# Scoring the first query tile against its own 128 keys, and adding a head's squares on VectorE before the ones-product

## The reference, cut to what matters

```
h = rmsnorm(x) * (1 + sc1) + sh1                 # sc1, sh1, ... = silu(c) @ w_ada + b_ada
proj = h @ w_in                                  # GLA q, k, v, gate; MoBA q, k, v; two branch gates
o_gla  = rmsnorm(gla(q, k, v, log_a)) * silu(gr) # 4 heads, dv = 256
o_moba = softmax(mask(q @ k.T * 128**-0.5)) @ v  # 8 heads x 128; 256 tokens are one block: plain causal
y = (sigmoid(gate_a) * (o_gla @ w_gla_out) + sigmoid(gate_b) * (o_moba @ w_moba_out)) @ w_o
x = x + gt1 * rmsnorm(y)
x = x + gt2 * rmsnorm(conv_ffn(rmsnorm(x) * (1 + sc2) + sh2))
```

## Time and profile before

| | |
|---|---|
| runs | 1500.78, 1501.9, 1497.0 us; median 1500.78 us |
| profiled execution | 1505.08 us, its span 1503.2 us |
| PE busy | 1442.4 us, 96% of the span |
| DVE busy | 1108.0 us, 74% |
| ACT busy | 756.1 us, 50% |
| POOL busy | 84.4 us, 6% |
| memory | 367 MB moved, mean 244 GB/s |

### The profile page before, as it was taken

How to read it: one execution, slowest core, us unless ns; L and a number is a source line. 1 busy time by engine, 2 the same in 40 slices (tenths; PEclk the granted TensorE clock), 3 DMA queues, 4 the chain that set the end, 5 groups by cost and what they waited for, 6 DMA issues and landing times.

```text
span 1503.2 us, 19959 instructions
## 1 busy us (share of the span) xinstructions
PE 1442.4 (96%) x7386; PEld 1231.6 (82%) x7386; DVE 1108.0 (74%) x1119; ACT 756.1 (50%) x743; POOL 84.4 (6%) x176
## 2 busy tenths in 40 slices
PE   2989999999999999999789999999999999999997
PEld 2777888888888888868678888888888888888886
DVE  5989978889898988855577778778777666545554
ACT  4443443353545365424566665665665665444443
POOL 3000001110101100000000000000000000000000
PEclk9999999999999999999989999999999999999999
DMA  9999979797989877866547677577765555555553
GB/s 361 387 329 354 313 230 327 243 308 260 304 265 299 266 253 254 305 227 235 168 168 237 225 237 236 194 240 236 236 237 184 191 180 193 192 195 195 195 195 112
DMA packets 235526, 367.03 MB, mean 244 GB/s; under 512 B 11455, under 2 KB 161473, under 8 KB 234706
## 3 DMA queue, kind: packets, MB, share of 16 engines
q1 hardware_dynamic: 215536, 294.69, 58.9%
q0 software_dynamic: 18848, 69.23, 12.8%
q10 hardware_dynamic: 1090, 2.40, 0.4%
HBM read 364.18 MB, written 2.10 MB: 244 GB/s over the span
## 4 chain that ended last, share of the span: by engine, by line
PE 82%; DVE 7%; DMA 7%; issue 2%; ACT 2%; SPq 0%; DVEq 0%
PE ps L1154 82%; DMA ada<-in_w_ada 3%; DVE lo L697 2%; DMA raw<-in_w_in 1%; DVE acc L707 1%; DVE acc_a L726 1%; ACT hi L426 1%; DMA adar<-in_w_ada 1%; DMA raw<-in_w_moba_out 1%; DVE acc_b L726 0%; DMA raw<-in_w_up 0%; DVE GA L817 0%; PE ps L1361 0%; DVE yo L1026 0%; DVE yt L1026 0%
## 5 line engine op out<-in xcount | busy, mean ns | idle before, releaser
L1154 PE MATMUL ps<-hT,hi 128*128 128x512 f32 x1936 | 469.0, 395 | 2.0 <-DVE hT L1066 2.0
L1154 PEld LDWEIGHTS ps<-hT,hi 128*128 128x128 f32 x1936 | 358.4, 189 | 74.1 <-issue 3.2
L426 ACT ACTIVATE hi<-raw 128x2048 fp32r<-128x2048 f32 x117 | 224.1, 1915 | 290.9 <-DMA raw<-in_w_in 192.9
L697 DVE TENSOR_TENSOR lo<-raw,hi 128x2048 fp32r<-128x2048 f32 x117 | 267.2, 2285 | 74.3 <-ACT hi L426 74.3
L1154 PEld LDWEIGHTS ps<-hT,lo 128*128 128x128 f32 x1936 | 248.2, 191 | 9.4
L1154 PE MATMUL ps<-hT,lo 128*128 128x256 f32 x1936 | 251.1, 283 | 0.0
L1115 DVE TENSOR_TENSOR lo<-raw,hi 128x2048 fp32r<-128x2048 f32 x88 | 200.1, 2291 | 50.1 <-ACT hi L658 50.0
L1154 PE MATMUL ps<-hi,hT 128*128 128x512 f32 x768 | 187.4, 397 | 8.2 <-DVE hT L751 5.7
L1154 PEld LDWEIGHTS ps<-hi,hT 128*128 128x128 f32 x768 | 144.5, 191 | 39.1 <-issue 9.0
L1154 PE MATMUL ps<-hi,asp 128*128 128x512 f32 x704 | 173.9, 389 | 0.0
L658 ACT ACTIVATE hi<-raw 128x2048 fp32r<-128x2048 f32 x88 | 166.2, 1906 | 4.4 <-DMA raw<-in_w_up 3.2
(11 more groups left out here) (199 smaller groups left out, 1334.9 us busy)
## 6 DMA issues: line engine op xcount, KB each, us to landing
raw<-in_w_up SPq DMA_DIRECT2D x176, 512.0 KB, 4.4
raw<-in_w_in SPq DMA_DIRECT2D x162, 512.0 KB, 5.6
ada<-in_w_ada POOLq DMA_DIRECT2D x128, 512.0 KB, 4.9
raw<-in_w_down SPq DMA_DIRECT2D x88, 512.0 KB, 4.1
adar<-in_w_ada SPq DMA_DIRECT2D x64, 512.0 KB, 9.7
raw<-in_w_o SPq DMA_DIRECT2D x32, 512.0 KB, 4.8
raw<-in_w_gla_out SPq DMA_DIRECT2D x16, 512.0 KB, 4.9
raw<-in_w_moba_out SPq DMA_DIRECT2D x16, 512.0 KB, 5.2
```

What stands on the lines that cost most here:

```text
L426: act.activation(hi[:, w % 4, :], raw[:, w % 4, :], ACT.Copy).then_inc(hi_done, 1)
L697: dve.tensor_tensor(lo[:, w % 4, :], raw[:, w % 4, :], hi[:, w % 4, :].bitcast(F32), ALU.subtract).then_inc(lo_done, 1)
L1154: return pe.matmul(out_, lhsT, rhs, start=start, stop=stop)
```

## The change

The scores of query tile 0 are computed against keys 0 to 127 alone. In `ssb` and in the bank a head now has 384 columns in place of 512: columns 0 to 127 for query tile 0, 128 to 383 for query tile 1 (`score_cols`). The mask is laid out anew, the row maximum is two instructions per `hd`, and the exponential, the scaling and the transposes follow the new columns. Apart from that, DVE adds the second half of the squares to the first in its tail at n = 0, and PE multiplies ones with that sum once. PE waits there for the new semaphore `sq_sum`, which DVE counts up, where it waited for ACT's `sq_done`.

```diff
+        def score_cols(qt):
+            return slice(0, P) if qt == 0 else slice(P, 3 * P)
...
             made(pool.memset(causal[:, :], 0.0))
-            cv4 = causal[:, :].rearrange("p (t k) -> p t k", t=TT)
-            made(pool.affine_select(out=cv4, in_=cv4, compare_op=ALU.is_ge, fill=-1e30, base=0,
-                                    pattern=[[P, TT], [-1, TOK]], channel_multiplier=1))
+            diagonal = causal[:, :].rearrange("p (t k) -> p t k", t=TT)[:, :, 0:P]
+            made(pool.affine_select(out=diagonal, in_=diagonal, compare_op=ALU.is_ge, fill=-1e30, base=0,
+                                    pattern=[[0, TT], [-1, P]], channel_multiplier=1))
...
                             for qt in range(TT):
-                                v = ssb[:, hd, TOK * qt:TOK * (qt + 1)]
+                                v = ssb[:, hd, score_cols(qt)]
                                 j = 2 * hd + qt
                                 act.activation(v, v, ACT.Exp, scale=SCALE, bias=stat[:, 20 + j:21 + j],
...
             def tail(prev, n):
+                if n == 0:
+                    dve.wait_ge(sq_done, prev + 1)
+                    dve.tensor_tensor(sq[:, 0, :], sq[:, 0, :], sq[:, 1, :], ALU.add).then_inc(sq_sum, 1)
                 if n == 1:
...
-                            link(dve.tensor_tensor(ssb[:, hd, :], ps[:, 6 + hd, :], causal[:, :], ALU.add))
-                            link(dve.reduce_max(stat[:, 16 + 2 * hd:18 + 2 * hd],
-                                                ssb[:, hd, :].rearrange("p (t k) -> p t k", t=TT), AX.X), wait=hd == 1)
+                            link(dve.tensor_tensor(ssb[:, hd, 0:3 * P], ps[:, 6 + hd, 0:3 * P], causal[:, 0:3 * P], ALU.add))
+                            for qt in range(TT):
+                                link(dve.reduce_max(stat[:, 16 + 2 * hd + qt:17 + 2 * hd + qt], ssb[:, hd, score_cols(qt)], AX.X),
+                                     wait=hd == 1 and qt == 1)
...
-                                v = ssb[:, hd, TOK * qt:TOK * (qt + 1)]
+                                v = ssb[:, hd, score_cols(qt)]
                                 j = 28 + 2 * hd + qt
                                 ins = dve.tensor_scalar(v, v, stat[:, j:j + 1], None, ALU.mult)
...
-                        for j, (qt, k) in enumerate(((0, 0), (1, 0), (1, 1))):
-                            ins = pe.transpose(ps[:, 6 + hd, P * j:P * (j + 1)],
-                                               ssb[:, hd, TOK * qt + P * k:TOK * qt + P * (k + 1)], ident[:, :])
+                        for j in range(3):
+                            ins = pe.transpose(ps[:, 6 + hd, P * j:P * (j + 1)], ssb[:, hd, P * j:P * (j + 1)], ident[:, :])
                         ins.then_inc(pt_done, 1)
-                    pe.wait_ge(sq_done, prev + 1)
-                    mm(ps[:, 5, 0:TOK], ones[:, :], sq[:, 0, :], True, False)
-                    mm(ps[:, 5, 0:TOK], ones[:, :], sq[:, 1, :], False, True).then_inc(ss_done, 1)
+                    pe.wait_ge(sq_sum, prev + 1)
+                    mm(ps[:, 5, 0:TOK], ones[:, :], sq[:, 0, :]).then_inc(ss_done, 1)
...
-                                ins = mm(ps[:, 6 + hd, TOK * qt:TOK * (qt + 1)], mqk[:, 0, hd, P * qt:P * (qt + 1)], mqk[:, 1, hd, :])
+                                ins = mm(ps[:, 6 + hd, score_cols(qt)], mqk[:, 0, hd, P * qt:P * (qt + 1)], mqk[:, 1, hd, 0:P * (qt + 1)])
```

More of the change, by code:

```diff
@@ L214, in layer_kernel @@
         cross, evac, vm_evac = sems("cross evac vm_evac")
-        e_ready, exp_done, level_ready, gram_done, select_done, a01_done = sems(
-            "e_ready exp_done level_ready gram_done select_done a01_done")
+        sq_sum, e_ready, exp_done, level_ready, gram_done, select_done, a01_done = sems(
+            "sq_sum e_ready exp_done level_ready gram_done select_done a01_done")
         av_done, ot_done, sq_done, ss_done, rs_done, tanh_done, og_f = sems(
```

## The result

The changed kernel takes 1521.52 us (median of 5 runs, 1519.97 to 1522.22) against 1500.78 us before (5 runs, 1497.0 to 1506.31): 20.7 us more, ratio 1.0112, 95% interval 1.0086 to 1.0139. The forecast was 1519.3 us. That the kernel is slower is clear of noise; by how much is known to a few us.

What follows compares the result with a forecast made beforehand. PE was taken to bound the kernel, DVE close behind. 16.5 us of waiting plus 4.5 of low clock less 2.5 of PE's work gave 18.5 us more: 1519.3 us median, 8 in 10 within 1509 to 1525 us.

Steps and rivals of the forecast that it cites:

- The wait: At each of the first three borders PE waits 5.5 us for DVE's sum of squares, 16.5 us in all.
- DVE's lateness: At the first three borders DVE reaches the add's place 5.34 us after PE wants the sum.
- DVE's shorter score work: Mask adds, row maxima and scalings on DVE before the border take 0.55 us less per head.
- No wait at the merge: At the border to the merge DVE's add is done about 1.8 us before PE wants it.
- The clock: PE's clock falls to half level at each of three border waits, costing 1.5 us each, 4.5 us in all.
- PE's saving: Shorter score products (0.24 us) and one ones-product fewer (0.38 us) save PE 0.62 us a head, 2.5 us in all.
- The rule that I had set aside: PE's score products: matmul distance proportional to columns alone would save 0.40 us a head, 3.1 us in the sum.
- The clock holds: Rival, chance 0.10: border stalls come without the 4.5 us of low clock; 14.0 us more, 1514.8 us.
- DVE keeps its lead: Rival, chance 0.07: only the first border stalls; 4.5 us more, 1505.3 us.
- PE is held there anyway: Rival, 0.06 with "The add comes in time": another wait already holds PE at the border product, only the difference costs.
- The add comes in time: Rival, 0.06 with "PE is held there anyway": border lateness falls under about 0.6 us, PE's saving remains, 1498.3 us.

Runs made afterwards that it cites:

- the repeat: The changed kernel itself, unaltered, timed again beside a kernel with 40 filling matmuls: 1522.4 us (6 runs), ratio 1.0123.
- the squares alone: Kernel before with only the edit to the sum: DVE adds the halves at n = 0, PE waits for it; 1522.8 us, ratio 1.0129.
- the scores alone: Changed kernel with the sum put back to two ones-products behind ACT's squares, shorter scores kept: 1501.16 us, ratio 0.9988.
- one border: Changed kernel with the sum on DVE at the first border only, two products at the others: 1508.21 us, ratio 1.0028.
- moved units: Changed kernel with three ada units per head (heads 0 to 2) moved from before the border to behind n = 3, 4, 5: 1500.59 us, ratio 0.999.
- the filled waits: Changed kernel with unused matmuls before PE's wait at three borders: 34 gave 1518.35 us, ratio 1.0097; 40 gave 1521.68 us, ratio 1.01.

## Why the prediction was right, and what was mis-sized

The mechanism came as forecast: three waits of nearly equal length, none at the merge, DVE's lead gone in each head. The number is within its range partly because the errors of the terms cancel: 0.6 us too much for the waits, 2.2 too little for the clock, 0.7 too little for the saving. With the measured terms the sum is 15.9 + 6.7 - 3.2 = 19.4 us, against 20.7 between the medians.

**The wait.** Forecast 3 x 5.5 = 16.5 us, measured 15.9 in the first profile, 15.3 in the repeat and 16.5 with the squares alone. The add takes 0.42 us as worked out from its neighbours, DVE's shorter score work gives 0.47 us a head (mask adds and maxima to the next instruction 2.35 us in place of 2.76, scalings to the split 0.98 in place of 1.04) where I had 0.55, and PE arrives 0.41 us earlier in place of 0.24. These would make 5.75 us a border; the mean is 5.3, so the term that was too large is the 5.34 of DVE's lateness. It isn't a constant: with the scores alone DVE starts the split of n = 0 at 4.6, 5.5 and 4.6 us behind PE's last transpose, where the kernel before has 5.3 each time. That the earlier trace rows agreed to 0.02 us was luck. The wait came three times, since DVE meets ACT's copy and PE again in each head; that the lateness comes from the units in front of the border, and that one border alone costs a third, the runs with moved units and with one border show. No wait at the merge: the add is done at 574.5, PE comes at 576.43.

**The clock.** This term was too small: 4.5 us forecast, 6.7 measured, 6.5 and 8.1 in the profiles of the repeated run and of the squares alone. The clock was low for about 3.4 us in the earlier trace rows, from 650.7 us on, all of it behind the wait. Here it was low from 327.2 to 334.1, from 412.6 to 416.0 and from 494.5 to 501.3 us: twice as long at two of the three borders (at two in the repeat, at all three with the squares alone). It did begin before the restart, by 0.3 to 2.2 us, as I had reckoned, but lasted 6.2, 3.1 and 4.6 us beyond it. Why some stretches are twice as long, the runs don't show. The page of the Trainium skill "TensorE: Matmul & The Clock Gate", section "HAM oscillation — how this bites in real kernels", has waits between bursts put each next burst at half rate; at all nine borders of the three profiles the trace agrees. As a part of the run time it is read from profiles; the filled waits confirm that it is there, and not its size.

**PE's saving.** Mis-sized too, by little. The eight loads of `mqk` now take 1.21 us to the next group, 0.15 each where I expected 0.17:

```profile
301.73 1.18 PEld L1161 LDWEIGHTS ps<-mqk 128*128 128x128 f32 x8
302.94 3.17 PEld L1161 LDWEIGHTS ps<-hT,hi 128*128 128x128 f32 x14
```

Against the 1.62 us of the earlier trace rows that is 0.41 us a head, the upper bound, since the products of `Mb` in the earlier trace rows were no price for these. With 0.41 for the scores and 0.38 for the product the saving is 3.2 us in place of 2.5. The rule that I had set aside, distance in proportion to the columns (the Trainium skill, page "TensorE: Matmul & The Clock Gate", section "Back-to-back issue gap"), gives 0.40; the trace has 0.41.

**The sum.** From the scores alone to the changed kernel the merge begins 21.8 us later (548.50 and 570.32): 15.9 of waiting + 6.7 of clock - 3 x 0.38 for the products = 21.5. From the kernel before it is only 18.3 us, because its profiled execution had a fall of the clock in the first head that the changed one hadn't, for 1.7 us, and because the kernel before lacks the 1.6 us that the scores save:

```profile
264.00:266.00 2.00, 2.00 (x9) 1.54 (x9) 2.00 (x3) 1.61 (x3) 0.00 (x0) 0.75 1.02 308
266.00:268.00 2.00, 2.00 (x6) 1.63 (x5) 2.00 (x4) 1.25 (x2) 0.00 (x0) 0.50 0.82 286
268.00:270.00 2.00, 2.00 (x12) 1.74 (x12) 2.00 (x6) 1.01 (x2) 0.53 (x1) 0.90 0.36 99
```

The rest of the way takes 951.2 us before and 949.3 after; nothing of size is given back there.

**The rivals.** "The clock holds" is wrong in every profile of the changed kernel. "DVE keeps its lead" and "PE is held there anyway" are wrong. "The add comes in time" is wrong here, and true with three units moved, where the waits are 0.5 us a border on average, under the 0.6 us of its condition.

## What to carry to other kernels

An engine can be late by most of a tile at no cost until another one asks it for something there. Before a small piece of work is moved from the bounding engine to one with idle time, look up in the timeline when the new engine reaches the very place in its queue and when the result is wanted; if it is late, move the piece ahead of the long work, which here made the same instructions 20 us cheaper. Saving 1.5 us of products is not worth a wait on an engine that itself waits for transfers.

## What the hardware showed beyond that

Waits of equal length end with and without a fall of the clock. In the first head the kernel before waits for `Mb` for 2.0 us and the clock falls at 265.0 us, 1.4 us after the restart; the changed kernel waits for 2.2 us at the same place and it holds. The wait of 2.97 us of the earlier trace rows had no fall; the same wait in the changed kernel, 2.92 us up to 761.3 us, has one that begins at 760.7. With the 2.83 us of the earlier trace rows, which had a fall, no length between 2 and 3 us tells the outcome. The nine waits at the borders, 4.4 to 5.7 us in the profiles of the changed kernel, its repeat and the squares alone, all had one.

The ada transfers land unevenly: DVE's wait for one at the first border was 2.06 us in one profile and 3.83 in another. Before the change PE did not feel it at the borders.
